# GpSimd holds its first transfers until the fourth tile of x has landed

## What is computed

```
def _rmsnorm(x, g):
    xf = x.astype(jnp.float32)
    y = xf * lax.rsqrt(jnp.mean(xf * xf, -1, keepdims=True) + NORM_EPS)
    return (y * g.astype(jnp.float32)).astype(x.dtype)

def _compress(x, pe, w, n_blk):
    b = x.shape[0]
    c = x[:, :(n_blk + 1) * CMP_STRIDE].reshape(b, n_blk + 1, CMP_STRIDE, x.shape[2], x.shape[3])
    first = jnp.einsum('bcjgd,jde->bcge', c + pe[:CMP_STRIDE, None, :], w[:CMP_STRIDE])
    second = jnp.einsum('bcjgd,jde->bcge', c + pe[CMP_STRIDE:, None, :], w[CMP_STRIDE:])
    return first[:, :n_blk] + second[:, 1:]
...
        h = _rmsnorm(x, g[0])
...
                pages = cache_nsa_kv[a][page_table]
                past = pages.reshape(pages.shape[0], -1, *pages.shape[3:])
...
    for j in range(CONV_WIDTH):
        conv = conv + conv_w[j] * gc[:, j:j + t]
```

## Time and profile before

| | us |
|---|---|
| median of 3 runs | 1977.71 |
| lowest and highest | 1976.08, 1978.95 |
| the profiled execution | 1976.04 |
| its span, first to last instruction | 1974.3 |

### The profile page before, as it was taken

One profiled execution on the slowest core, in us unless ns is written; L12 is line 12 of the kernel. 1 busy time (PEld: TensorE's weight loads), 2 busy tenths in 40 slices (PEclk: granted clock), 3 DMA queues, 4 the chain that ended last, 5 costly groups with the idle time before them and its releaser, 6 DMA issues. The chain is left out here.

```text
span 1974.3 us, 34666 instructions
## 1 busy us (share of the span) xinstructions
PE 1744.6 (88%) x13374; PEld 1405.1 (71%) x13390; DVE 823.2 (42%) x1476; ACT 617.4 (31%) x1104; POOL 598.7 (30%) x448
## 2 busy tenths in 40 slices
PE   5999959888969996999999976999869699999996
PEld 4578746666758874788887854888647478888785
DVE  2744436555423235554442243200763554444223
ACT  3522322222211125433331244222343533333121
POOL 3124401111100013655562422332021455555330
PEclk9999958889967688999999986999779899999998
DMA  9423263000044211232343211222421123334211
GB/s 221 129 65 86 73 169 129 1 0 0 1 133 144 65 43 43 76 106 86 99 120 89 76 37 24 86 76 74 134 69 44 43 86 96 102 88 129 75 47 46
DMA packets 223076, 158.49 MB, mean 80 GB/s; under 512 B 12540, under 2 KB 216989, under 8 KB 222645
## 3 DMA queue, kind: packets, MB, share of 16 engines
q1 hardware_dynamic: 221118, 151.41, 26.3%
q0 software_dynamic: 1856, 5.70, 1.3%
HBM read 146.39 MB, written 19.02 MB: 84 GB/s over the span
## 5 line engine op out<-in xcount | busy, mean ns | idle before, releaser
L275 POOL TENSOR_TENSOR wlo<-wst,whi 128x1024 bf16<-128x1024 f32 (+1 forms) x180 | 427.5, 2379 | 704.2 <-ACT whi L264 704.1
L291 PE MATMUL ps<-hhi,whi 128*128 128x272 f16 x1664 | 466.5, 280 | 10.7 <-PEq L178 5.7
L292 PE MATMUL ps<-hlo,whi 128*128 128x272 bf16 x1664 | 466.5, 280 | 0.0
L293 PE MATMUL ps<-hhi,wlo 128*128 128x272 f16 x1664 | 466.3, 280 | 0.0
L264 ACT CAST whi<-wst 128x1024 f16<-128x1024 f32 (+1 forms) x180 | 196.5, 1102 | 205.3 <-PE ps L293 200.4
L291 PE MATMUL ps<-whi,hhi 128*128 128x256 f16 (+1 forms) x720 | 196.6, 273 | 5.5 <-PEq L178 3.8
L291 PE MATMUL ps<-g_hi,whi 128*128 128x272 f16 x704 | 198.0, 281 | 0.0
L292 PE MATMUL ps<-g_lo,whi 128*128 128x272 bf16 x704 | 198.0, 281 | 0.0
L293 PE MATMUL ps<-g_hi,wlo 128*128 128x272 f16 x704 | 198.0, 281 | 0.0
L293 PE MATMUL ps<-whi,hlo 128*128 128x256 f16 (+1 forms) x720 | 196.2, 273 | 0.0
L292 PE MATMUL ps<-wlo,hhi 128*128 128x256 bf16 (+1 forms) x720 | 196.2, 273 | 0.0
(11 more groups left out here) (372 smaller groups left out, 2900.7 us busy)
## 6 DMA issues: line engine op xcount, KB each, us to landing
wst<-in_ffn_w_up SPq DMA_DIRECT2D x88, 512.0 KB, 3.9
wst<-in_ffn_w_down SPq DMA_DIRECT2D x32, 704.0 KB, 4.7
wst<-in_gla_w_in SPq DMA_DIRECT2D x24, 512.0 KB, 3.7
wst<-in_nsa_w_in SPq DMA_DIRECT2D x20, 512.0 KB, 3.8
out_win_s<-in_state_win_kv SPq DMA_DIRECT2D x8, 1016.0 KB, 14.3
chunks<-in_cache_nsa_kv SPq DMA_DIRECT2D x16, 256.0 KB
chunks<-in_cache_nsa_kv POOLq DMA_DIRECT2D x16, 256.0 KB, 21.5
wst<-in_nsa_w_o SPq DMA_DIRECT2D x8, 512.0 KB, 3.9
```

Source lines behind the costliest of these rows:

```text
L275: pool.tensor_tensor(core.wlo[:, k, 0:w], core.wst[:, k, 0:w], core.whi[:, k, 0:w], ALU.subtract).then_inc(core.w_lo, 1)
L291: pe.matmul(out, a_hi, b_hi, start=start and j == 0, stop=False)
L292: pe.matmul(out, a_hi, b_lo, start=False, stop=False)
L293: last = pe.matmul(out, a_lo, b_hi, start=False, stop=stop and j == n - 1)
```

## The change

More of the change, by code:

```diff
@@ L802, in _ @@
             def _(pool):
+                pool.wait_ge(x_in[3], 16)
                 taps.load(pool)
```

## The result

The changed kernel takes 1985.49 us in the median of 20 runs (1978.78 to 1990.2), the kernel before 1979.11 in the median of 20 (1966.85 to 1982.02). The ratio is 1.0038 with a 95% interval from 1.0025 to 1.0051: slower by 7.5 us, between 5 and 10. The forecast was 1984.7 and +7.0.

The account below looks back on a forecast made before the run. Bound: transfers, then TensorE's in-order work. Tile 4 at 14.3 plus 19.4 puts the rows at 33.7, line 711 +7.0 us; 1976.04 becomes 1983.0, plus 1.67 for the median 1984.7 us. Range 1978.7 to 1990.5.

Parts of the forecast that it names:

- What bounds the kernel: First stage: transfers first, then engine work; TensorE's line 711 and the x chain meet at 31.46 us.
- What x gains: Loads of x on SP's queue: at 268 GB/s alone, the fourth tile lands at 14.3 us, 7.5 us sooner.
- What the rows lose: GpSimd's queue: first issue at 14.3 instead of 1.41, 19.4 us to the last row, rows landed at 33.7.
- The middle piece: GpSimd's loads from first landing to eighth weight load: 12.6 us before, scaled by 0.72 to 9.1 us.
- What is hidden: First stage: weights for line 725 land before the rows, pages are in time, SP's first weight load doesn't feel the change.
- TensorE's clock: Compression in the first stage: the clock's rise moves with the work; 1 to 2 us if it doesn't.
- (a): Rival, GpSimd's queue keeps its issue pace: rows land at 27.7, +1.0 us, 1978.7; chance 0.16.
- the formula: A gain by a formula that the given text doesn't define, nor its place or size; chance 0.03.
- (b): Rival, GpSimd's old pace of 23.7 us remains: rows land at 38.0, +11.3 us, 1989.0; chance 0.15.
- (c): Rival, SP's own queue sets x's pace: tile 4 stays at 21.8, +14.5 us, 1992.2; chance 0.04.
- The time: Whole kernel: profiled 1976.04 us with +7.0 is 1983.0; with the median's 1.67 above, 1984.7 us.
- a shift at 107 us that isn't found at the end: Sign of a wrong prediction: the next stage's shift, forecast to start at 113.8 instead of 106.81, missing at the kernel's end.

Follow-up runs that it names:

- after_again: The changed kernel run once more with no edit, on one chip with the kernel before: 1985.69 us (median of 12) beside 1977.64, ratio 1.0033.

## Why the prediction was right

- *What bounds the kernel.* TensorE's line 711 was taken as the meeting point of two chains, with 1.5 us of cover on the rows. The bracket of 17.93 us behind the last row's transfer is that, and with the rows ahead of the weights the loss of the whole change goes away in the timed runs.
- *What x gains* was undersized. The fourth tile was put at 14.3 and landed at 12.2. Of these 2.1 us, 1.4 are the first tile, which was left at 6.5 and landed at 1.7 + 3.4 = 5.1; the other 0.7 are the pace. The 268 GB/s were read in the 1.8 us before GpSimd's data came; alone, SP's queue moved 2.95 MB between 2.6 and 12 us, 314 GB/s:

```profile
q1 hardware_dynamic: 969, 2.95, 101.6%
```

- *What the rows lose* was undersized as well, and the other way: 19.4 us were taken from first issue to last row, 22.2 were measured. Its pieces were put at 5.3, 9.1 and 5.0 and measured 7.0 (the first load), 8.6 (28.0 - 19.4) and 6.6. The middle piece, the one that was scaled, was right within half a microsecond. The first and the last were too short: the first was taken over from the kernel before, where it was 5.3, and the rows' own piece was put below its old 5.8. That the middle piece came out right is luck. The packets beside pages ran at 119 in 3 us, 39.7 a microsecond, not 49, while the weights passed (20 to 23 us), and at 531 in 11 us, 48.3, only later on (35 to 46 us). Scaled by 35.5/39.7, the middle piece would have been put at 11.3 us:

```profile
q0 software_dynamic: 119, 0.35, 65.8%
...
q0 software_dynamic: 531, 1.72, 65.3%
```

- The two errors cancel, by luck: x came 2.1 us sooner than forecast and the rows took 2.8 us longer. 33.7 was forecast for the rows, 34.6 measured, and the shift at line 711 was 8.1 instead of 7.0.
- *What is hidden.* Weights, pages and SP's weight blocks cost nothing, as said: the compression starts at 60.22, right behind line 725, and GpSimd's eighth page lands at 48.6 (forecast 47.3). One reading was off without a price: SP, forecast to come to its first block at 45.74 as before, was there sooner and did wait for line 711's end, and issued the block at 39.62.
- *TensorE's clock.* That its rise in the compression moves with the work, at 1 to 2 us if it doesn't, was the author's estimate. In the first trace it came earlier relative to the work (the four page transposes at 65.00 take 0.60 us; their twins before, at 58.35, took 1.06), which gave back 2.0 us (and 0.5 more before it, as some of the normalised tiles were turned at the higher clock: granted 0.67 from 40 to 50 us, against 0.50 in after_again); in after_again only 0.4. What was missed is the second place, the fall behind the stage's end, which took 2.6 us in the first trace and 1.7 in the second (granted 0.71 and 0.83 from 112 to 122 us). The prediction named no change there. Whether the fall belongs to the change's price isn't shown: both traces of the kernel with the rows ahead of the weights have it too (2.6 and 1.7 us, +2.3 against before at 120 us in both), and its time is that of before.
- *The rivals.* (a), the queue at issue pace, is what the engines do without SP's pages (12.9 us); with them it doesn't hold. The chances also carry 0.03 for a gain by "the formula". No run shows that gain or a formula for it: the loads of 128 KB landed 3.0 to 4.4 us after issue with SP's pages out of the way and 6.9 to 10.7 beside them. (b), the old pace, was the nearer one for the queue: 22.2 us against 23.7, and 22.3 in the run with the short hold. (c) fell clearly: the fourth tile came 9.6 us sooner.
- *The time.* +8.1 us at line 711, less 0.4 to 2.5 up to the next stage, plus 1.7 to 2.6 for the fall of the clock behind it, makes 8.2 and 9.4 at 115 us in the two traces, and +7.5 us (5 to 10) over all runs. Over the rest of the kernel executions of one program drift apart by several us, the slower ones at a lower mean clock: 0.903 to 0.895 over the 20 runs. So one of the prediction's own signs of being wrong, a shift at 107 us that isn't found at the end, did show in the first trace (5.6, then 2.6 at 1800 us), and it was a poor sign to name: a single trace of this kernel can't give the sign of a change of 0.3% at its end. At line 711 it gives the shift to about half a microsecond (34.75, 34.78 and, with the transposes at the end, 35.22), at the next stage only to 2 us.

## What to carry to other kernels

Before a transfer is held back to let another pass, look for who waits first on the engine that runs in order: here the small rows (0.45 MB of GpSimd's 5.7) were queued behind a megabyte of weights and stood ahead of the normalised x on TensorE, so hastening x by 9.6 us made TensorE's work behind it 8 us later. Put what is consumed first first in its own queue, and hold only what has measured slack. When two queues share the DMA engines, size a late start by the landing times that the loads had beside other traffic, not by an empty machine.

## What the runs showed that was not expected

- The column of the granted clock read 1.00 for the first 60 us of the kernel before, though four page transposes took 1.06 us there and 0.60 from 60.73 on the earlier trace rows. In the changed kernel, whose transposes went faster for a while around 12 us (next point), the same column reads 0.53 from 14 to 34 us and 0.63 from 46 to 69. So in the kernel before the column tells nothing of the first 60 us; the duration of one form of matmul does.
- The changed kernel has an early rise that the kernel before doesn't show: with the second to fourth tile turned one right behind the other, TensorE ran the last two at a higher clock (16 transposes in 2.67 us from 10.60, and in 3.19 from 10.70 in after_again, where 8 took 1.97 before). It had lost it again before the rows came: granted 0.50 from 20 to 40 us, and line 711 took 4.85 us.
- Six row loads of together 0.45 MB, beside x, delayed the fourth tile from 12.2 to between 17.6 and 19.6 us in four traces. At the 314 GB/s that SP's queue had alone, their bytes would be 1.4 us (an estimate), so sharing the engines cost x several times what the rows weigh.
